# Rotary partners by a VectorE shuffle, and the mLSTM running maximum spread by one rounded product

## The reference

```python
def partial_rope(x, cos, sin):                      # first block: 8 + 8 of 64 features of a head
    half = ROPE_DIM // 2
    x1, x2 = x[..., :half], x[..., half:ROPE_DIM]
    rot = jnp.concatenate([x1 * cos - x2 * sin, x2 * cos + x1 * sin], axis=-1)
    return jnp.concatenate([rot, x[..., ROPE_DIM:]], axis=-1)

def _rotate(u, c, s):                               # second block: 16 + 16, twice in a head
    half = u.shape[-1] // 2
    u1, u2 = u[..., :half], u[..., half:]
    return jnp.concatenate([u1 * c - u2 * s, u2 * c + u1 * s], axis=-1)

# mLSTM: weights against a maximum per query row
m_row = jnp.maximum(inter, jnp.max(d_intra, axis=-1))
w_intra = jnp.exp(d_intra - m_row[..., None])
s = jnp.einsum('bhcld,bhcsd->bhcls', q, k) * w_intra
```

## Time and profile before

| | us |
|---|---|
| median of 3 runs | 2984.29 |
| lowest and highest run | 2984.26, 2986.93 |
| the profiled execution's own time | 2982.44 |
| its span, first to last instruction | 2980.7 |
| PE busy | 2903.7 (97% of the span) |
| VectorE busy | 1374.1 (46%) |
| ScalarE busy | 1129.2 (38%) |
| GpSimd busy | 12.8 |
| DMA, mean over the span | 85 GB/s |

### The profile page before, as it was taken

How to read it: one execution, slowest core, us unless ns; L and a number is a source line. 1 busy time by engine, 2 the same in 40 slices (tenths; PEclk the granted TensorE clock), 3 DMA queues, 4 the chain that set the end, 5 groups by cost and what they waited for, 6 DMA issues and landing times. The chain is left out here.

```text
span 2980.7 us, 41276 instructions
## 1 busy us (share of the span) xinstructions
PE 2903.7 (97%) x17398; PEld 2441.4 (82%) x17398; DVE 1374.1 (46%) x1891; ACT 1129.2 (38%) x1612; POOL 12.8 (0%) x23
## 2 busy tenths in 40 slices
PE   8999999989999999999999998999999999999998
PEld 7888888778888888888888777888888878888887
DVE  3333355575333354333345676233354367555541
ACT  3233344544223254322244544222245355434430
POOL 0000000000000000000000000000000000000000
PEclk9999999999999999999999999999999999999999
DMA  4333412103233421233412103233431201213331
GB/s 150 99 93 131 134 34 64 34 3 114 82 95 113 141 100 57 93 98 126 143 34 64 46 3 107 78 96 95 149 121 49 75 23 38 99 61 95 99 123 54
DMA packets 71479, 254.50 MB, mean 85 GB/s; under 512 B 8056, under 2 KB 9208, under 8 KB 71296
## 3 DMA queue, kind: packets, MB, share of 16 engines
q1 hardware_dynamic: 71296, 251.87, 26.1%
HBM read 249.74 MB, written 2.10 MB: 84 GB/s over the span
## 5 line engine op out<-in xcount | busy, mean ns | idle before, releaser
L211 PE MATMUL ps<-h_hi,w_space 128*128 128x512 f32 (+1 forms) x5056 | 1448.6, 370 | 2.9 <-DVE h_lo L309 2.9
L211 PEld LDWEIGHTS ps<-h_hi,w_space 128*128 128x128 f32 x5056 | 919.5, 189 | 164.4 <-DVE h_lo L309 3.7
L199 DVE TENSOR_TENSOR w_space<-w_raw,w_space 128x1024 fp32r<-128x1024 f32 x440 | 533.8, 1224 | 1033.0 <-ACT w_space L192 1032.7
L211 PE MATMUL ps<-h_lo,w_space 128*128 128x512 f32 (+1 forms) x2528 | 931.6, 368 | 0.0
L192 ACT CAST w_space<-w_raw 128x1024 fp32r<-128x1024 f32 x440 | 455.9, 1048 | 908.9 <-PE ps L211 551.0
L221 PE MATMUL ps<-w_space 128*128 128x512 f32 x3312 | 767.6, 394 | 13.6 <-DVE w_space L199 11.3
L221 PEld LDWEIGHTS ps<-w_space 128*128 128x128 f32 x3312 | 626.8, 190 | 144.8 <-issue 13.8
L211 PEld LDWEIGHTS ps<-h_lo,w_space 128*128 128x128 f32 x2528 | 478.1, 189 | 78.5 <-issue 1.4
L586 ACT CAST w_space<-act_p 128x512 fp32r<-128x512 f32 x88 | 54.7, 621 | 192.0 <-DVE act_p L598 175.8
L601 DVE TENSOR_TENSOR w_space<-act_p,w_space 128x512 fp32r<-128x512 f32 x88 | 60.9, 693 | 70.7 <-ACT w_space L586 70.7
L598 DVE TENSOR_TENSOR act_p<-act_s,ps 128x512 f32<-128x512 f32 x88 | 59.9, 681 | 47.5 <-PE ps L211 47.5
(11 more groups left out here) (395 smaller groups left out, 2237.6 us busy)
## 6 DMA issues: line engine op xcount, KB each, us to landing
w_raw<-in_w_ffn_in SPq DMA_DIRECT2D x176, 512.0 KB, 3.5
w_raw<-in_w_ffn_out SPq DMA_DIRECT2D x88, 512.0 KB, 3.6
w_raw<-in_w_in SPq DMA_DIRECT2D x64, 512.0 KB, 3.5
w_raw<-in_w_up SPq DMA_DIRECT2D x44, 512.0 KB, 3.5
w_raw<-in_w_out SPq DMA_DIRECT2D x24, 512.0 KB, 4.0
w_raw<-in_w_down SPq DMA_DIRECT2D x22, 512.0 KB, 3.5
w_raw<-in_w_ple_gate SPq DMA_DIRECT2D x16, 512.0 KB, 3.5
gain_pre<-in_gains_pre SPq DMA_DIRECT2D x10, 512.0 KB, 4.8
```

Source lines behind the costliest of these rows:

```text
L199: nc.vector.tensor_tensor(self.lo(n), self.raw[:, n % SLOTS, :], self.hi(n).bitcast(F32), ALU.subtract).then_inc(self.lo_ready, 1)
L211: m = nc.tensor.matmul(c.ps[:, bank, t], part[:, cols], moving[:, k, t], start=(k == 0 and i == 0), stop=(k == KD - 1 and i == 2))
```

## The change

1. The matrices `rope_turn` and `axial_turn` go, and with them all 15 partner products on TensorE and the waits around them. VectorE makes the partner itself with a `stream_shuffle` of the 128x512 tile, which permutes the partitions in each group of 32, into the buffer `turned_sin`; the product with the sine then reads that buffer instead of a PSUM bank. The sign of the partner goes into the tables (`inv_freq` is negated for the first eight features of a head, the sine table of the second block for the first sixteen of each 32).
2. The running maximum is kept as a rounded part on partitions 0 to 3 and a rest on partitions 32 to 35 of one fp32r tile, `run_parts`, whose other partitions are zero. ScalarE makes the rounded part and a rounded copy of the selectors, VectorE the rest, GpSimd clears the tile. `spread_max` becomes one fp32r product of 36 rows.
3. The constant matrices' DMA carries 128x896 instead of 128x1152 numbers, the selectors' DMA 36x512 instead of 4x768.

```diff
@@ WindowAttention
-    def partner(self, pe, nc, i):
-        c = self.c
-        self.wait_tile(pe, AK_T + i)
-        nc.tensor.matmul(c.ps[:, self.PARTNER_BANK[i], :], c.mat["rope_turn"], c.proj[:, AK_T + i, :],
-                         start=True, stop=True).then_inc(self.turned, 1)
@@ tensor_after
-        if n == 4:
+        if n == 6:
             pe.wait_ge(c.consts_loaded, 48)
-            self.partner(pe, nc, 0)
-            self.partner(pe, nc, 1)
-        if n == 5:
-            self.partner(pe, nc, 2)
-        if n == 6:
             self.wait_tile(pe, AV_T)
...
-            if h == 0:
-                pe.wait_ge(self.roped, 2)
-            if h == 0:
-                pe.wait_ge(self.v_copied, 1)
-                self.partner(pe, nc, 3)
-            if h == 1:
-                pe.wait_ge(self.roped, 4)
-                self.partner(pe, nc, 4)
             self.scores(pe, nc, h)
@@ rotate
+        nc.vector.stream_shuffle(self.turned_sin[:, :], u, ROPE_PARTNER).then_inc(self.turned, 1)
         nc.vector.tensor_tensor(self.rotated[:, :], u, c.rope[:, 0, :], ALU.mult).then_inc(self.cos_done, 1)
         dve.wait_ge(self.turned, i + 1)
-        nc.vector.tensor_tensor(self.turned_sin[:, :], c.ps[:, self.PARTNER_BANK[i], :], c.rope[:, 1, :],
+        nc.vector.tensor_tensor(self.turned_sin[:, :], self.turned_sin[:, :], c.rope[:, 1, :],
                                 ALU.mult).then_inc(self.sin_done, 1)
@@ recurrence_stage
+                nc.gpsimd.memset(run_parts[:, :].bitcast(F32), 0.0).then_inc(run_cleared, 1)
...
                     if h == 0:
                         pe.wait_ge(u_copied, 1)
+                        pe.wait_ge(run_split, 1)
...
-                    nc.tensor.matmul(c.ps[:, MAX_BANK, :], select[:, h, :], run_max, start=True, stop=True).then_inc(max_spread, 1)
+                    nc.tensor.matmul(c.ps[:, MAX_BANK, :], select_r[:, h, :], run_parts[:, :], start=True,
+                                     stop=True).then_inc(max_spread, 1)
...
                 rows_of(0)
+                act.wait_ge(run_cleared, 1)
+                nc.scalar.copy(run_hi, run_max).then_inc(run_first, 1)
+                act.wait_ge(loaded, 48)
+                nc.scalar.copy(select_r[:, :, :], select[:, :, :]).then_inc(run_first, 1)
...
                 dve.wait_ge(loaded, 48)
+                dve.wait_ge(run_first, 2)
+                nc.vector.tensor_tensor(run_lo, run_max, run_hi.bitcast(F32), ALU.subtract).then_inc(run_split, 1)
                 masks_of_a(0)
@@ HeadNorm
-        if 9 <= n < 9 + self.NA:
-            t = n - 9
-            pe.wait_ge(self.normed, t + 1)
-            if t >= 2:
-                pe.wait_ge(self.sin_done, t - 1)
-            nc.tensor.matmul(c.ps[:, self.PARTNER_BANKS[t % 2], :], c.mat["axial_turn"], c.proj[:, t, :], start=True,
-                             stop=True).then_inc(self.turned, 1)
...
+        nc.vector.stream_shuffle(self.turned_sin[:, t % 2, :], c.proj[:, t, :], AXIAL_PARTNER).then_inc(self.turned, 1)
         nc.vector.tensor_tensor(self.rotated[:, t % 2, :], c.proj[:, t, :], c.rope[:, 0, :], ALU.mult).then_inc(self.cos_done, 1)
         dve.wait_ge(self.turned, t + 1)
-        nc.vector.tensor_tensor(self.turned_sin[:, t % 2, :], c.ps[:, self.PARTNER_BANKS[t % 2], :], c.rope[:, 1, :],
+        nc.vector.tensor_tensor(self.turned_sin[:, t % 2, :], self.turned_sin[:, t % 2, :], c.rope[:, 1, :],
                                 ALU.mult).then_inc(self.sin_done, 1)
```

More of the change, by code:

```diff
@@ L52 @@
 NVEC2 = _at
-MATS = ("ident", "ones", "halves", "rope_turn", "swap", "axial_turn", "strict_low", "strict_up", "incl_up", "causal")
+MATS = ("ident", "ones", "halves", "swap", "strict_low", "strict_up", "incl_up", "causal")
 class Stage:
@@ L963 @@
 HEADS, GROUP, WIN = 8, 4, 128
+ROPE_PARTNER = [(i + 8) % 16 + 16 * (i // 16) for i in range(32)]
+AXIAL_PARTNER = [(i + 16) % 32 for i in range(32)]
 class WindowAttention:
@@ L3267, in shape_matrices @@
     same_half, same_chunk = row // DH == col // DH, row // CHUNK == col // CHUNK
[L3268 to L3281 removed]
+    m = {"ident": row == col, "ones": (row >= 0) & (col >= 0), "halves": same_half,
+         "swap": (row + DH) % P == col, "strict_low": same_chunk & (row > col),
          "strict_up": same_chunk & (row < col), "incl_up": same_chunk & (row <= col), "causal": row <= col}
@@ L3346, in layouts @@
     a["window_masks"] = np.where(np.concatenate([blocks[:, 0:2], by_key[:, None, :2 * WIN]], 1), 0.0, NEG).astype(np.float32)
-    sel = np.zeros((4, 6, P), np.float32)
-    for h in range(4):
-        sel[h, h] = 1.0
-        sel[h, 4 + h // 2, DH * (h % 2):DH * (h % 2) + DH] = 1.0
+    sel = np.zeros((SPREAD_ROWS, M_HEADS, P), np.float32)
+    for h in range(M_HEADS):
+        sel[[h, 32 + h], h] = 1.0
     a["selectors"] = sel
```

32 lines of the change are left out of this document (9 added, 23 removed).

## The result

The changed kernel takes **2966.76 us** (median of 4 runs, 2965.41 to 2970.55) against 2984.28 (2983.67 to 2986.93) for the kernel before in the same batch: ratio 0.995, 95% interval 0.9938 to 0.9963. Forecast were 2970.5 and 2965 to 2976. The profiled execution took 2970.55 us (span 2968.8), 11.9 less than that of before.

A forecast was written before the change was run, and what follows sets the result against it. TensorE, busy for 2903.7 of 2980.7 us, was taken as the bound. Terms 7.0 + 4.3 + 2.5 = 13.8 us off the profiled 2982.44 gave 2968.6, plus 1.85 to the median: 2970.5 us, range 2965 to 2976.

The forecast's parts named there:

- Partners, first block (7.0): First block's attention: ten partners off TensorE give each layer 4.3 less 0.8 us of new waits, 7.0 us together.
- head 0's two meetings: First block: TensorE waits 0.4 us for VectorE at head 0's rough scores and 0.4 at its first diagonal product.
- the slope: First block: a shuffle x us longer than 0.60 costs each layer 3x more, three early shuffles preceding the diagonal.
- The shuffle (0.60 us of queue): VectorE: each 128x512 shuffle takes 0.60 us of queue, like a float32 product of that shape; range 0.35 to 1.23.
- Axial partners (4.3): Second block's head normalisation: five partners off TensorE save 4.3 us with no new wait; steps 6.8 us instead of 7.7.
- Spread, heads 0 to 3: Recurrence stages: heads 1 and 2 gain 0.63 us each, head 3 nothing, head 0 at most 0.3; both stages 2.5.
- Spread, the start of the stage: Recurrence stage: casts and subtraction delay TensorE's first-mask wait by 0.1 to 0.2 us; with head 0's 0.3 it nets 0.
- Constants (0): Start of the kernel: the smaller constants' DMA lies under the first feed-forward part and changes the time by 0.
- 1.85 above it, which I carry over: Whole kernel: the median of runs lies 1.85 us above the profiled execution, so 2968.6 becomes 2970.5 us.
- Clock: Recurrence stages: one or two short 1.2 GHz stretches more or fewer, plus or minus 3 us, no sign known.
- the rival in which the clock takes part back: Recurrence: four more stretches at 1.2 GHz cost 6 us, giving 2976.5 us; chance 0.09.
- all of it counts: Head 0's waits don't come and all eight spreads pay in full: 17.9 us, 2966.4 us; chance 0.16.

The follow-up runs named there:

- The doubled shuffle: Against the changed kernel, each rotation of the first block makes its shuffle twice, the second after a wait for the first: 2972.50 us.
- the places filled: Against the changed kernel, matrix products that nobody reads in three idle TensorE places behind each recurrence stage: 2968.85 us.

## Why the prediction was right, and where it was off

- *Partners, first block (7.0).* Right in every step. TensorE's slots went; the waits at head 0's two meetings came at 0.40 and 0.45 us, forecast 0.4 each; a layer gave 3.5. The chain behind the first rotation is right too: the weight unit starts 0.5 us earlier than before, counted from that rotation (forecast 0.4), and the first diagonal 0.1 us later (forecast 0.2). The doubled shuffle shows the slope.
- *The shuffle (0.60 us of queue).* It is 0.62 to 0.64, and 0.73 to 0.75 long. The value taken from a product of the same shape was right within 0.04. The queue time agrees with the estimate of 0.6 us from the Trainium skill (VectorE: DVE Perf Modes, section on the perf-mode tier table); the duration in the trace is 0.13 to 0.15 longer.
- *Axial partners (4.3).* Right; the head sums of line 2191 come 6.82 us apart where it was 7.70, the kernel before first:

```profile
2341.23 0.60 PE L2198 MATMUL ps<-mats,dense_wide 128*128 128x128 f32 x4
...
2348.93 0.60 PE L2198 MATMUL ps<-mats,dense_wide 128*128 128x128 f32 x4
```

```profile
2340.16 0.60 PE L2191 MATMUL ps<-mats,dense_wide 128*128 128x128 f32 x4
...
2346.98 0.60 PE L2191 MATMUL ps<-mats,dense_wide 128*128 128x128 f32 x4
```

- *Spread, heads 0 to 3.* Right head by head: 0.31, 0.63, 0.63, 0; the 36-row product costs its lower bound, a slot of 0.43 of which 0.19 to 0.20 is the change of shape.
- *Spread, the start of the stage: the step that failed.* "They are done at 570.3", said of the two casts, took for granted that the selectors lie there when ScalarE asks; the late selectors were named as a risk, but the sum put the start at nothing. The cast begins with the landing, the first mask 1.44 us behind it, and TensorE's 0.1 to 0.2 us became 0.6 at like landing. So the 2.5 us are 1.9 by this sum; the time measured for the spread alone, 2.0 ± 0.7, allows both. In the profiled pair the first mask of the first stage starts 2.5 us later than before, counted from the stage's first transpose (5.82 against 3.30 us), where 0.7 was forecast: part of that is a later landing, and whether the larger selectors cause it is open.
- *Constants (0).* Perhaps too low a cost: the 0.8 us ahead of the first rotation named above, which no run isolates.
- *Sum and total.* 13.8 at equal clock, by chance as close as it is, since the spread's 0.6 lies within the scatter; the profiled pair, both at 0.990, is 11.9 apart. The median came 3.7 us lower than forecast. That is the step "1.85 above it, which I carry over": the runs of before shown then all stood near 2984.3, its mean at a granted 0.990. Over the 53 executions beside the experiments its median is 2981.62, below the profiled 2982.44, so nothing of that offset is the kernel's. The changed kernel's runs at 0.990 average 2971.2, those at 0.991 and 0.992 2967.3 and 2966.0, and 7 of its 9 were of the latter.
- *Clock.* Forecast was plus or minus 3 us with no sign. In the profiled pair the two recurrence stages, from the first transpose to the next feed-forward part, went from a granted 0.93 to 0.95 and from 0.96 to 0.93, at the edge of the 0.03 that was named, and the second came out 1.2 us longer. At equal clock none of the 13.8 is missing and the mean clocks are alike, so the rival in which the clock takes part back is not borne out. Nor is "all of it counts": the waits came, and head 3's spread gave nothing. The rule cited there (the Trainium skill, TensorE: Matmul & The Clock Gate, Part 1), by which activity releases the lower level, did not help to lift it: with the places filled the two windows of 10 us behind the first stage have a granted 0.84 and 0.65, without filling 0.93 and 0.55, the same mean. Whether less work on TensorE brought more time at the lower level is not shown either way.

## What to carry to other kernels

Where TensorE has no idle time, the gain of removing one of its instructions is its start-to-start slot, less what the engine that takes over is late at the next meeting; add that engine's queue up to the meeting. A cast or a split that is put at a stage's start must not make urgent work depend on the slowest of its loads: give each load its own semaphore, and issue first what is needed first. That the urgent work waits for the slowest load is shown here; the gain from separate semaphores is 2.0 ± 1.4 us, with a cast moved at the same time. When a forecast carries an offset from a profiled execution to a median, three runs are too few if the time goes with the granted clock of the run.

## What the runs showed of the hardware that was not expected

- The granted clock of a whole execution varies for one and the same kernel, between 0.990 and 0.992 in 53 executions of the kernel before and between 0.989 and 0.993 in six of the doubled shuffle, and each 0.001 goes with 2.0 us of 2970.
- The clock fell to 1.2 GHz in a stretch in which TensorE was busy for 9.95 of 10 us, and for 11.44 of the 15 us ahead of it.
- Small loads issued at a stage's start (12 to 160 KB) took 2.3 to 4.3 us until their user could start. No run separates the part of their size.
- Each shuffle is preceded on VectorE by a row of its own, a mask load of 8 to 17 ns.
